# Attention pairs: first two score products between the latent value tiles, rotary keys copied by ScalarE, low part of the first output weights behind the pairs

## The reference, cut to what matters

```python
q = (rmsnorm(c_q, q_norm_g) @ w_uq).reshape(b, tp, MLA_HEADS, MLA_QK_DIM)
q_mla = concatenate([q[..., :64], rope(q[..., 64:], pos)])
kv = (rmsnorm(c_kv, kv_norm_g) @ w_ukv).reshape(b, tp, MLA_HEADS, 64 + 64)
k_mla = concatenate([kv[..., :64], broadcast(rope(k_r, pos), MLA_HEADS)])   # one rotary key for all heads
v_mla = kv[..., 64:]
o_mla = causal_block_attention(q_mla, k_mla, v_mla)
# per query: index scores, the 128 best keys, softmax over these alone
o_dsa = indexed_sparse_attention(rope(q_s), rope(k_s), v_s, rope(q_i), rope(k_i), w_i, topk)
h = h + concatenate([o_mla, o_dsa]) @ w_o
```

## Time and profile before

| | us |
|---|---|
| median of 3 runs | 1753.06 |
| lowest and highest | 1750.89, 1755.3 |
| the profiled execution's own time | 1754.76 |
| its span in the trace | 1752.8 |
| PE busy | 1678.9 |
| DVE busy | 1008.3 |
| ACT busy | 676.2 |
| POOL busy | 590.2 |

### The profile page before, as it was taken

How to read it: one execution, slowest core, us unless ns; L and a number is a source line. 1 busy time by engine, 2 the same in 40 slices (tenths; PEclk the granted TensorE clock), 3 DMA queues, 4 the chain that set the end, 5 groups by cost and what they waited for, 6 DMA issues and landing times.

```text
span 1752.8 us, 22905 instructions
## 1 busy us (share of the span) xinstructions
PE 1678.9 (96%) x9216; PEld 1341.5 (77%) x9216; DVE 1008.3 (58%) x1524; ACT 676.2 (39%) x965; POOL 590.2 (34%) x203
## 2 busy tenths in 40 slices
PE   7999999999999998999999999998999999999997
PEld 6777788888788886777788877686677788887876
DVE  4256545686988889985563654897963222222123
ACT  5473223334344355445333323425663322222122
POOL 1422013343633342000244432333774344443432
PEclk8999999999999999999999999998999999999999
DMA  5223002335655665555744322112002233332322
GB/s 165 83 96 96 1 11 89 95 96 143 154 119 136 139 141 106 105 115 163 244 135 128 88 70 73 48 43 85 2 1 73 79 90 96 96 96 74 100 83 81
DMA packets 267566, 168.14 MB, mean 96 GB/s; under 512 B 88875, under 2 KB 247814, under 8 KB 267334
## 3 DMA queue, kind: packets, MB, share of 16 engines
q1 hardware_dynamic: 240544, 142.80, 30.2%
q10 hardware_dynamic: 26614, 22.25, 4.8%
q0 software_dynamic: 304, 1.65, 0.3%
HBM read 145.15 MB, written 16.78 MB: 92 GB/s over the span
## 4 chain that ended last, share of the span: by engine, by line
PE 79%; DVE 11%; ACT 3%; issue 2%; DMA 2%; ACTq 1%; POOL 1%; SPq 0%; DVEq 0%; POOLq 0%
PE PS L700 22%; PE PS L701 22%; PE PS L702 22%; DVE ring_lo L1960 2%; PE PA L896 1%; PE PA L893 1%; ACTq L1621 1%; PE PA L874 1%; PE PS L1260 1%; PE PS L1272 1%; PE PA L1106 1%; PE PA L1244 1%; POOL ring_lo L2639 1%; DVE PB L2563 1%; ACT ring_hi L1382 1%
## 5 line engine op out<-in xcount | busy, mean ns | idle before, releaser
L2639 POOL TENSOR_TENSOR ring_lo<-ring,ring_hi 128x2048 fp32r<-128x2048 f32 (+2 forms) x93 | 405.6, 4361 | 965.9 <-ACT ring_hi L1382 965.5
L1382 ACT ACTIVATE ring_hi<-ring 128x2048 fp32r<-128x2048 f32 (+2 forms) x123 | 223.2, 1821 | 209.5 <-PE PS L702 171.8
L700 PE MATMUL PS<-U3h,ring_hi 128*128 128x512 f32 x352 | 140.0, 398 | 3.1 <-POOL ring_lo L2639 3.1
L701 PE MATMUL PS<-U3l,ring_hi 128*128 128x512 f32 x352 | 140.6, 399 | 0.0
L702 PE MATMUL PS<-U3h,ring_lo 128*128 128x512 f32 x352 | 139.5, 396 | 0.0
L2599 DVE TENSOR_TENSOR SF<-PS,rs 128x512 f32<-128x512 f32 x22 | 15.2, 691 | 166.7 <-PE PS L702 166.6
L700 PE MATMUL PS<-HT5h,ring_hi 128*128 128x512 f32 x256 | 106.3, 415 | 3.0 <-DVE ring_lo L1960 2.9
L1960 DVE TENSOR_TENSOR ring_lo<-ring,ring_hi 128x2048 fp32r<-128x2048 f32 x30 | 91.6, 3065 | 27.6 <-ACT ring_hi L1382 27.6
L702 PE MATMUL PS<-HT5h,ring_lo 128*128 128x512 f32 x256 | 101.4, 396 | 0.0
L701 PE MATMUL PS<-HT5l,ring_hi 128*128 128x512 f32 x256 | 101.2, 395 | 0.0
L1870 ACT ACTIVATE SF<-SF 128x512 f32<-128x512 f32 x22 | 13.9, 632 | 179.1 <-DVE SF L2599 179.1
(11 more groups left out here) (486 smaller groups left out, 4224.9 us busy)
## 6 DMA issues: line engine op xcount, KB each, us to landing
ring<-in_gla_w_in SPq DMA_DIRECT2D x20, 1024.0 KB, 5.2
ring<-in_s_w_in SPq DMA_DIRECT2D x16, 1024.0 KB, 5.8
ring<-in_s_w_glu SPq DMA_DIRECT2D x16, 1024.0 KB, 5.9
ring<-in_w_gate SPq DMA_DIRECT2D x22, 512.0 KB, 4.0
ring<-in_w_up SPq DMA_DIRECT2D x22, 512.0 KB, 5.3
ring<-in_w_down SPq DMA_DIRECT2D x16, 704.0 KB, 4.4
ring<-in_w_in SPq DMA_DIRECT2D x9, 1024.0 KB, 5.2
ring<-in_gla_w_out SPq DMA_DIRECT2D x8, 1024.0 KB, 5.8
```

The lines of the kernel that those rows point to most:

```text
L700: pe.matmul(dst, w[0], x[0], start=start, stop=False)
L701: pe.matmul(dst, w[0], x[1], start=False, stop=False)
L1382: act.activation(ring_hi[:, n % NSLOT, 0:plan.size[n]], ring[:, n % NSLOT, 0:plan.size[n]], ACT.Copy)\
L2639: pool.tensor_tensor(ring_lo[:, n % NSLOT, at], ring[:, n % NSLOT, at], ring_hi[:, n % NSLOT, at].bitcast(F32), ALU.subtract).then_inc(wlo ...
```

## The change

It has seven parts.

1. The rotary key is turned ahead of the sparse keys (`ROTATIONS`), and ACT copies it to the heads' rows of Km in four instructions between the query tiles (`rotary_keys`), in place of one DVE instruction.
2. PE forms S(0) and S(1) between the value tiles. The wait for the last value tiles moves from S(0) to T(0).
3. ACT does the exponentials of pair 0 between the first and the second value tile.
4. DVE's selection rounds go from pairs 1 to 24 to pairs 3 to 26.
5. The first output weights: ACT makes the high part behind pair 24's exponentials and the copy of T(22), POOL the low part behind all pairs.
6. T(31) goes to the banks PA and waits for no copy.
7. The scaling of pair 31 moves from POOL to DVE.

```diff
@@ ROTATIONS
+        ROTATIONS += [(KR[:], MNOPE, MQK, 0, R_MC, tiles["kk"][0])]
+        KEYS_TURNED = len(ROTATIONS)
         ROTATIONS += [(KS[:, j, :], 0, P, 0, R_C, tiles["ks"][j]) for j in range(4)]
-        ROTATIONS += [(KR[:], MNOPE, MQK, 0, R_MC, tiles["kk"][0])]
...
+        def turned_banks(p):
+            return PA if p == len(PAIRS) - 1 else PS
+        OUT_SPLIT, FIRST_CHOICE = len(PAIRS) - 8, 3
@@ TensorE
             def scored(p):
                 if p == 0:
                     pe.wait_ge(ro_read, len(ROTATIONS))
                     pe.wait_ge(roped, len(ROTATIONS))
-                    for tile in tiles["ukvv"][-2:]:
-                        read_out(pe, tile)
...
+            EARLY = 2
             for i, tile in enumerate(tiles["ukvv"]):
...
                 m.then_inc(tile_done, 1)
+                if i < EARLY:
+                    scored(i)
...
             def transposed(p):
-                if p > 0:
-                    pe.wait_ge(pT_sb, p)
-                if i + 2 > 4 and p >= 2:
-                    pe.wait_ge(oa_ready, p - 1)
+                if p == 0:
+                    for tile in tiles["ukvv"][-2:]:
+                        read_out(pe, tile)
+                to = turned_banks(p)
+                if to is PS:
+                    if p > 0:
+                        pe.wait_ge(pT_sb, p)
+                    if i + 2 > 4 and p >= 2:
+                        pe.wait_ge(oa_ready, p - 1)
...
-            for p in range(len(PAIRS) + 3):
+            for p in range(EARLY, len(PAIRS) + 3):
@@ ScalarE
+            def rotary_keys(j):
+                ins = act.activation(Km[MNOPE:MQK, 2 * j:2 * j + 2, :],
+                                     KR[MNOPE:MQK, :].unsqueeze(1).broadcast_to([MROPE, 2, T2]), ACT.Copy)
+                if j == 3:
+                    ins.then_inc(kr_copied, 1)
             for i, tile in enumerate(tiles["uqr"]):
                 evac(tile, QR[:, i, :], scale=-MQK ** -0.5)
+            act.wait_ge(roped, KEYS_TURNED)
+            rotary_keys(0)
             for i, tile in enumerate(tiles["uqn"]):
...
+                if i < 3:
+                    rotary_keys(i + 1)
...
-            split_weights(tiles["attn_out"][0].loads[0])
...
+            for i, tile in enumerate(tiles["ukvv"]):
+                if i == 1:
+                    exponentials(0)
+                act.wait_ge(tile_done, tile.t + 1)
...
             for p in range(len(PAIRS) + 2):
-                if p < len(PAIRS):
+                if 0 < p < len(PAIRS):
                     exponentials(p)
                 if p >= 2:
                     copy_transposed(p - 2)
+                if p == OUT_SPLIT:
+                    split_weights(tiles["attn_out"][0].loads[0])
@@ VectorE
-                if n == FIRST_QR - 1:
-                    dve.wait_ge(roped, FIRST_QR)
-                    dve.wait_ge(tile_done, tiles["vs"][-1].t + 1)
-                    dve.tensor_copy(Km[MNOPE:MQK, :, :], KR[MNOPE:MQK, :].unsqueeze(1).broadcast_to([MROPE, MH, T2])).then_inc(kr_copied, 1)
...
-                if 0 < p <= 3 * TOPK // 16:
+                if 0 <= p - FIRST_CHOICE < 3 * TOPK // 16:
                     select(1)
...
-            for p in range(len(PAIRS) - 4, len(PAIRS)):
+            output(len(PAIRS) - 4)
+            for n in (2 * len(PAIRS) - 2, 2 * len(PAIRS) - 1):
+                dve.wait_ge(p_ready, n)
+                dve.wait_ge(rsum_ready, n + 1)
+                nk = keys(PAIRS[n // 2][1])
+                ts(PB[:, n % 6, 0:nk], PB[:, n % 6, 0:nk], mx[:, n % 6, 2:3], None, ALU.mult).then_inc(p_ready, 1)
+            for p in range(len(PAIRS) - 3, len(PAIRS)):
                 output(p)
@@ GpSimd
-            split_weights(tiles["attn_out"][0].loads[0])
-            for n in range(2 * MH * NPAIR):
+            split_weights(tiles["ukvv"][0].loads[0])
+            for n in range(2 * MH * NPAIR - 2):
```

More of the change, by code:

```diff
@@ L1207, in pe_program @@
                     rotate(FIRST_QR + i)
[L1208 to L1219, removed]
             def scored(p):
@@ L1247, in scored @@
                 m.then_inc(score_ps, 1)
+            EARLY = 2
+            w = parts_view(tiles["ukn"][0].loads[0], (MH * P,))
+            pe.wait_ge(pad_zero, 4)
+            for i, tile in enumerate(tiles["ukn"]):
+                feature_tile(tile, lambda k: both(w, slice(None), slice(i * P, (i + 1) * P)),
+                             lambda k: (CKh[:, 0:T2], CKl[:, 0:T2]), 1, T2)
+            for i, tile in enumerate(tiles["ukvv"]):
+                open_tile(tile)
+                for b in range(2 if i < 2 else 1):
+                    t0 = (2 * i + b) * P
+                    m = product(PS[:, 2 * tile.slot + b, :], (CKh[:, t0:t0 + P], CKl[:, t0:t0 + P]),
+                                both(w, slice(None), slice(MH * MNOPE, MH * P)), True, True)
+                m.then_inc(tile_done, 1)
+                if i < EARLY:
+                    scored(i)
             def transposed(p):
                 i = PAIRS[p][1]
-                if p > 0:
-                    pe.wait_ge(pT_sb, p)
-                if i + 2 > 4 and p >= 2:
-                    pe.wait_ge(oa_ready, p - 1)
+                if p == 0:
[7 more added lines that the diff above has]
+                        pe.wait_ge(oa_ready, p - 1)
                 for h in range(2):
@@ L1819, in act_program @@
                 ins.then_inc(slot_free[tile.slot], 1)
-            for i, tile in enumerate(tiles["ukvv"]):
-                act.wait_ge(tile_done, tile.t + 1)
-                nb = 2 if i < 2 else 1
-                act.activation(Vm[:, 2 * i:2 * i + nb, :], PS[:, 2 * tile.slot:2 * tile.slot + nb, :], ACT.Copy).then_inc(slot_free[tile.slot], 1)
-            split_weights(tiles["attn_out"][0].loads[0])
             def exponentials(p):
@@ L1831, in exponentials @@
                                    accum_out=mx[:, n % 6, 1:2]).then_inc(exp_ready, 1)
+            for i, tile in enumerate(tiles["ukvv"]):
+                if i == 1:
+                    exponentials(0)
+                act.wait_ge(tile_done, tile.t + 1)
+                nb = 2 if i < 2 else 1
+                act.activation(Vm[:, 2 * i:2 * i + nb, :], PS[:, 2 * tile.slot:2 * tile.slot + nb, :], ACT.Copy).then_inc(slot_free[tile.slot], 1)
             def copy_transposed(p):
                 i = PAIRS[p][1]
+                of = turned_banks(p)
                 act.wait_ge(pT_ps, p + 1)
@@ L1838, in copy_transposed @@
                 n = min(i + 2, 4) * P
-                ins = act.activation(PT2[p % 2][:, :, 0:n], PS[:, 0:2, 0:n], ACT.Copy)
+                ins = act.activation(PT2[p % 2][:, :, 0:n], of[:, 0:2, 0:n], ACT.Copy)
                 if i + 2 > 4:
-                    ins = act.activation(PT2[p % 2][:, :, n:n + P], PS[:, 2 + p % 2, 0:2 * P].rearrange("p (h n) -> p h n", h=2), ACT.Copy)
+                    ins = act.activation(PT2[p % 2][:, :, n:n + P], of[:, 2 + p % 2, 0:2 * P].rearrange("p (h n) -> p h n", h=2), ACT.Copy)
                 ins.then_inc(pT_sb, 1)
             for p in range(len(PAIRS) + 2):
-                if p < len(PAIRS):
+                if 0 < p < len(PAIRS):
                     exponentials(p)
```

2 lines of the change are left out of this document (1 added, 1 removed).

## The result

| | changed kernel | kernel before, run beside it |
|---|---|---|
| median, first comparison | 1748.58 us (1745.39 to 1751.70, 8 runs) | 1753.83 us (1750.89 to 1755.50, 8 runs) |
| ratio | 0.9971, 95% interval 0.9960 to 0.9982 | |
| profiled execution, its own time | 1747.89 us, span 1745.8 | 1754.76 us, span 1752.8 |

By the ratio the change is worth 5.1 us (3.2 to 7.0 by the interval), where 5.2 were forecast, and the median is 0.7 above the 1747.9 of the prediction. The same kernel, run again beside others, gave a ratio of 0.9966 (0.9953 to 0.9978). So the size is right; whether the steps are is for the traces to say.

A forecast was written before the change was run, and what follows sets the result against it. PE, busy 96% of the span, was taken as the bound, so time comes off only where it waits or runs slowly; -6.2 + 1.4 - 0.4 + 0.4 - 0.4 = -5.2 us gave 1747.9 us, range 1744.8 to 1752.0.

The forecast's parts named there:

- Part 1, the start: Start of the pairs, without POOL's weights ahead and with key copies on ACT: R(4) at 1213.5 instead of 1219.71, -6.2 us.
- Rival C: Key copies on ACT are dear, 1.9 us each, ACT late by 4.5: sum -1.5 us, 1751.5 us; chance 0.08.
- Part 2, the clock: PE's clock at the start of the pairs: one fall of the shorter kind, 3.3 us, costing +1.4 us (ends 0 and +3).
- rival A: The clock holds at the start of the pairs: sum -6.6 us, 1746.5 us; chance 0.25.
- Part 3, the selections: DVE's selections at pairs 3 to 26: -0.4 us from fewer wide ones, +0.4 us from late-pair waits up to T(27).
- Pile-up B: Late pairs from 1275, where PE bounds: two DVE selections of 1.54 show in full, -2.5 us, 1750.5 us; chance 0.15.
- Part 4, the end: End: T(31) goes to other banks and DVE scales pair 31, so the first output matmul comes 0.4 us earlier, -0.4.
- Rival D: Slower: PE stays at 1.2 GHz through the narrow pairs, +8.4 us, 1761.5 us; chance 0.05.

## Why the prediction was right, and where it was not

- **Part 1, the start: -6.2, measured -5.71** with the clock held. The mechanism and its order were right down to the PE gap behind S(3) and to the late exponentials as its cause. Counted from the common zero the gap was forecast from 22.4 to 24.4 and found from 23.4 to 24.9, and T(0) came 0.97 later than forecast, T(1) 0.49. 1.50 of the 5.71 are the clock, low before and not here; the forecast of part 1 was for full clock too, and so has it in. What was mis-sized is the price of ACT's copies: 1.08 us each and not 0.98, so that the latent keys come 1.34 late and not 0.8. That is the missing half microsecond: 0.4 of it by the four durations alone. Rival C (1.9 us each) is out.
- **Part 2, the clock: +1.4.** As a figure it is close: 0, 1.23, 1.24 and 3.02 in four profiles, 1.4 in the mean. As a step it was wrong: it took the order of the work to decide whether the clock falls, and forecast and rival A turned out to be two executions of one kernel. In the first profile A came true (its -6.6 against -6.22 at the output matmuls), in the second the long fall (-3.20), and the median lies between. Four profiles are too few to say what the clock costs in the median. The estimate from the earlier trace rows for a fall of 3.3 us was good, 1.4 against 1.23.
- **Part 3, the selections: -0.4 and +0.4, measured -0.53 and +0.50.** R(27) came 5.0 us behind R(26) (5.25 forecast) and S(26)'s wait of 0.66 went. But the waits that came in are not the forecast one, T(26) for ACT's copy: T(25) waits 0.81 and T(27) 0.34, both for DVE's output copies, which the prediction did not have in the path. 0.81 + 0.34 - 0.66 = 0.49 is the 0.50; that it lies near +0.4 is luck. Pile-up B didn't come: of the 3.1 us of selection only 0.50 showed. The high part of the output weights on ACT cost nothing: the kernel with the selections at 1 to 24 has it and takes 27.21 us from R(24) to R(31), exactly as the kernel before, which doesn't.
- **Part 4, the end: -0.4, measured -0.48**, all of it from T(31)'s banks. The prediction named DVE's scaling beside them; it has no share. It also named ACT's copy of T(30) as the wait that goes; the one that ended last was DVE's output copy of pair 29, and the size came out right because the other banks lift both.
- **Rival D** has nothing for it: from every fall here the clock came back ahead of R(8), still in the narrow pairs.
- The profile's sum is -5.71 - 0.53 + 0.50 - 0.48 = -6.22, which is 126.71 - 120.49. That the total of -5.2 hit the median owes something to chance, since part 1 was 0.5 too good, and since the cost of the clock differs by 3 us between executions.

## What to carry to other kernels

Before an engine is given a side job (here 4.5 us of weights on POOL, 4.3 us of key copies on ACT), ask who waits for that engine next, and put the job where its engine idles with nobody queued behind it. When a hole has been opened, ask which chain is next (here ACT's, which took 1.0 of the 4.0 us at once), and count the clock that PE has there: a fall costs more the more work of PE lies in it, and the same 10.2 us at half clock took 0.93 us more once the hole was filled. A change of 0.3% is judged by traces that are lined up at an event ahead of the edit, since one fall of the clock moves a run by 0.6 to 2.6 us. And where the trace names a releaser that had ended well ahead of the wait's end, look in the program for the other semaphores that the instruction waits for.

## What the runs showed that I had not expected

- The granted clock differs between executions of one program at the same instruction: no fall, one of 3.4 us, or one of 6.9 us, behind the same gap. It also fell ahead of the value tiles, 13.0 to 14.8 us behind the VS evacuation, in three of the seven profiles with the key copies on ACT, at a cost of 0.56 to 0.81 us, and in none of the seven others. With the copies on ACT PE waits 1.36 us there for the last Qm copy of ACT, and 0.43 without them. What exactly brings a fall stays open.
- A copy of 32 partitions x 1056 elements takes ACT 1.08 us, as long as 1.06 for 128 x 1024: the few partitions save nothing. DVE does all four in one instruction of 2.35.
- A matmul of 128x256 on operands that aren't split takes 0.48 us, as long as two of 128x512 with split ones (0.233 us each).
